# A two-block transformer on one core: starting the second block's stages with a pair of weight units in token layout, tile by tile

## The reference

```python
h = h + 0.5 * rmsnorm_2(swiglu(rmsnorm_2(h, g[0]), ffn1_w_in[i], ffn1_w_out[i]), g[1])
u = rmsnorm_2(h, g[2])
mix = even_mixer(u, ...) if i % 2 == 0 else odd_mixer(u, ...)
h = h + rmsnorm_2(mix, g[3])
h = h + 0.5 * rmsnorm_2(swiglu(rmsnorm_2(h, g[4]), ffn2_w_in[i], ffn2_w_out[i]), g[5])
gate = jax.nn.sigmoid(h @ ple_w_gate[i])
h = h + rmsnorm_2(gate * (p[i] @ ple_w_proj[i]), g[6])
```

## Time and profile before

| | |
|---|---|
| runs, us | 1816.14, 1817.77, 1819.4; median 1817.77 |
| span of the profiled execution, us | 1812.1; no time of its own beside it is given |
| PE busy | 1772.9 us, 98% |
| DVE, ACT busy | 952.5 us, 53%; 718.8 us, 40% |
| mean granted clock of PE | 0.998 of full speed |
| chain that ended last | PE 86%, DVE 7%, ACT 4%, DMA 1% |

### The profile page before, as it was taken

The page is one execution under the profiler, slowest core; times in us unless marked ns, Lnnn a source line. Parts: engine busy times, 40 slices in busy tenths (PEclk is TensorE's granted clock), DMA queues, the critical chain, the costliest instruction groups (busy, mean ns, idle before and its releaser), DMA issues.

```text
span 1812.1 us, 24884 instructions
## 1 busy us (share of the span) xinstructions
PE 1772.9 (98%) x9912; PEld 1349.9 (74%) x9912; DVE 952.5 (53%) x1200; ACT 718.8 (40%) x949; POOL 41.3 (2%) x55
## 2 busy tenths in 40 slices
PE   9999999999999999999999999999999999999997
PEld 8886454444545488888988888788887879888886
DVE  6584111111111275665776566675666854566665
ACT  5562111111111254435665344653445345444444
POOL 2000000000000000000000000000000001200000
PEclk9999999999999999999999999999999999999999
DMA  9367899999999955554435555545555554555551
GB/s 291 105 251 304 333 423 422 422 422 422 421 422 422 362 197 186 186 187 153 140 115 182 186 185 186 187 151 190 189 189 166 180 168 140 202 164 186 185 186 58
DMA packets 191205, 428.75 MB, mean 237 GB/s; under 512 B 7292, under 2 KB 145632, under 8 KB 166560
## 3 DMA queue, kind: packets, MB, share of 16 engines
q1 hardware_dynamic: 187952, 418.41, 63.5%
q0 software_dynamic: 3184, 9.36, 1.6%
HBM read 426.69 MB, written 1.05 MB: 236 GB/s over the span
## 4 chain that ended last, share of the span: by engine, by line
PE 86%; DVE 7%; ACT 4%; DMA 1%; issue 1%; DVEq 0%; SPq 0%; POOL 0%; ACTq 0%
PE pw L494 62%; PE acc L494 22%; DVE wl L1716 2%; DMA raw<-in_w_in 1%; PE pw L856 1%; ACT arena L1387 1%; DVE x L2158 0%; ACT sm L1379 0%; ACT wh L1214 0%; ACT arena L1495 0%; DVE scr L2170 0%; ACT L1238 0%; DVE scr L2227 0%; ACT arena L1514 0%; DMA cB<-in_decays 0%
## 5 line engine op out<-in xcount | busy, mean ns | idle before, releaser
L494 PE MATMUL pw<-aa,wh 128*128 128x512 f32 (+1 forms) x2384 | 702.4, 359 | 5.1 <-DVE aa L1726 2.7
L494 PE MATMUL pw<-aa,wl 128*128 128x256 f32 x1960 | 551.3, 281 | 0.0
L1716 DVE TENSOR_TENSOR wl<-raw,wh 128x2048 fp32r<-128x2048 f32 x205 | 463.2, 2297 | 110.5 <-ACT wh L1214 107.6
L494 PEld LDWEIGHTS pw<-aa,wh 128*128 128x128 f32 x2384 | 421.5, 190 | 82.3 <-DVE wl L1716 4.6
L1214 ACT ACTIVATE wh<-raw 128x2048 fp32r<-128x2048 f32 x205 | 380.9, 1906 | 51.4 <-DMA raw<-in_odd_w_in 28.5
L494 PEld LDWEIGHTS pw<-aa,wl 128*128 128x128 f32 x1960 | 371.9, 190 | 1.4
L494 PE MATMUL acc<-wh,aa 128*128 128x512 f32 x1088 | 347.0, 392 | 5.7 <-DVE aa L1734 3.5
L494 PE MATMUL pw<-mring,arena 128*64 128x512 f32 x1520 | 334.9, 595 | 5.4 <-issue 5.4
L494 PEld LDWEIGHTS pw<-mring,arena 128*64 128x64 f32 x1520 | 107.4, 137 | 206.7 <-issue 204.4
L494 PEld LDWEIGHTS acc<-wh,aa 128*128 128x128 f32 x1088 | 204.2, 188 | 52.1 <-DVE wl L1716 3.9
L494 PE MATMUL acc<-wl,aa 128*128 128x512 f32 x544 | 212.0, 390 | 0.0
(11 more groups left out here) (408 smaller groups left out, 1250.5 us busy)
## 6 DMA issues: line engine op xcount, KB each, us to landing
raw<-in_ffn_w_in SPq DMA_DIRECT2D x88, 1024.0 KB, 5.1
mring<-in_w_ed SPq DMA_DIRECT2D x64, 1024.0 KB, 16.4
mring<-in_w_eg SPq DMA_DIRECT2D x63, 1024.0 KB, 16.1
mring<-in_w_eu SPq DMA_DIRECT2D x63, 1024.0 KB, 18.1
raw<-in_ffn_w_out SPq DMA_DIRECT2D x44, 1024.0 KB, 5.0
raw<-in_odd_w_in SPq DMA_DIRECT2D x24, 1024.0 KB, 5.2
raw<-in_w_in SPq DMA_DIRECT2D x12, 1024.0 KB, 10.3
raw<-in_even_w_in SPq DMA_DIRECT2D x11, 1024.0 KB, 5.5
```

What stands on the lines that cost most here:

```text
L494: return pe.matmul(out, lhs, rhs, start=start, stop=stop, skip_group_check=True)
L1716: dve.tensor_tensor(wl[:, u % RING, :], raw[:, u % RING, :], wh[:, u % RING, :].bitcast(F32), ALU.subtract).then_inc(sig(f"{ep}_lo"), 1)
```

## The change

From the second stage on that starts with a norm after a tile-wise product (both stages of feed-forward two, feed-forward one of layer 1 and the odd mixer), the first two weight units are computed as a pair in token layout: activations stationary, 512 weight columns of two units streamed, tile 0 first, then tile 1 (`turn_tile`, `pair_tile`). High and low parts are made for one tile at a time, 128 columns an instruction, and those of tile 0 are written in between tile 1's norm steps. The matmuls of zeros are gone there. In the feed-forwards the pair is gate and up of the first block; its activation is done in token layout and turned by four transposes. In the odd mixer the pair is the values of head 0 (`ODD_ORDER`), copied out by ACT. The embedding stage does embeddings, turning and gates tile by tile; tile 0's gates end before tile 1's begin, and x of tile 0 is squared and normed before tile 1's sigmoid.

```diff
-        ODD_ORDER = (0, 1, 2, 3, 4, 5, 6, 7, 16, 8, 9, 10, 11, 12, 13, 14, 15, 17, 18, 19, 20, 21, 22, 23)
+        ODD_ORDER = (9, 8, 0, 1, 2, 3, 4, 5, 6, 7, 16, 10, 11, 12, 13, 14, 15, 17, 18, 19, 20, 21, 22, 23)
...
+            def turn_tile(t, spare):
+
+                w.more("diag_ready")
+                for c in range(KC):
+                    last = mm(tile_turned(t, c, spare), x[:, t, c * P:(c + 1) * P], diag[:, t, :])
+                    if c in (0, 1, 4, 7):
+                        last.then_inc(sig("turned"), 1)
+
+            def pair_tile(ep, u, t, bank, slots):
+
+                unit_ready(ep, u + 1)
+                out = pw[:, bank + t, :].rearrange("p (a n) -> p a n", a=2)
+                for k in range(KC):
+                    w.more("act_ready")
+                    last = mm3(out, ah[:, k, tok(t)], al[:, k, tok(t)], wh[:, slots, k * 256:(k + 1) * 256],
+                               wl[:, slots, k * 256:(k + 1) * 256], k == 0, k == KC - 1)
+                return last
...
-                turn_normed({0: (29, 0), 2: (28, 0)}.get(idx, (0, 14)))
-                pairs_of("b", u0, 0, arriving=True).then_inc(sig("b_used"), 1)
-                pairs_of("b", u0 + 1, 2).then_inc(sig("b_used"), 1)
...
+                    slots = slice(u0 % RING, u0 % RING + 2)
+                    turn_tile(0, 0)
+                    pair_tile("b", u0, 0, 2, slots).then_inc(sig("psum_for_act"), 1)
+                    turn_tile(1, 0)
+                    pair_tile("b", u0, 1, 2, slots).then_inc(sig("b_used"), 2)
...
+                    if by_tile:
+                        w.more("dve_for_pe", 2)
+                        for c in range(2):
+                            for t in range(NT):
+                                turned = pe.transpose(acc[:, 0, c * T + t * P:c * T + (t + 1) * P], hid_rows[:, t, c * P:(c + 1) * P], ident)
+                        turned.then_inc(sig("psum_for_act"), 1)
...
                 w.more("act_ready")
-                rows("b", UB[(l, "ple_proj")], 12, True, True, final=True, dst=pw, tile="proj_tile")
-                w.more("x_ready")
...
+                weighted(v0, 12, 0, pw[:, 0:2, :], True, True).then_inc(sig("psum_for_act"), 1)
+                w.more("dve_for_pe")
+                turn_plain(0)
+                weighted(v0, 12, 1, pw[:, 2:4, :], True, True).then_inc(sig("b_used"), 1)
+                w.more("dve_for_pe")
+                w.more("pp_ready")
+                turn_plain(1)
+                w.more("act_ready", KC)
+                for j in range(4):
+                    last = weighted(v0 + 1 + j, 2 * j, 0, acc[:, 0:2, :], j == 0, j == 3)
+                last.then_inc(sig("first_tile"), 1)
+                for j in range(4):
+                    w.more("act_ready", 2)
+                    weighted(v0 + 1 + j, 2 * j, 1, acc[:, 2:4, :], j == 0, j == 3).then_inc(sig("b_used"), 1)
...
+                slots = slice(0, RING, RING - 1)
+                turn_tile(0, 2)
+                pair_tile("b", u0, 0, 0, slots)
+                turn_tile(1, 2)
+                pair_tile("b", u0, 1, 0, slots).then_inc(sig("b_used"), 2)
...
-                for p in range(8):
-                    if p >= 2:
+                for p in range(2, 10):
+                    if p == 3:
+                        w.more("proj_evac")
+                    if p >= 4:
                         w.more("qk_evac")
...
+            def high_tile(t, chunks, col, spare):
+
+                for c in chunks:
+                    if c in (0, 1, 2, 5):
+                        w.more("turned")
+                    act.activation(ah[:, c, tok(t)], tile_turned(t, c, spare), ACT.Copy, scale=col(c)).then_inc(sig("high"), 1)
...
+                    split("b", u0 + 2)
+                    split("b", u0 + 3)
+                    for t in range(NT):
+                        if t == 0:
+                            w.more("psum_for_act")
+                        else:
+                            used("b", u0 + 1)
+                        act.activation(gate_tok[:, t, :], pw[:, 2 + t, 0:256], ACT.Silu).then_inc(sig("act_for_dve"), 1)
+                    split("b", u0 + 4)
...
+                        if between:
+                            high_tile(0, (half,), col, spare)
                     sum_root(t, factor)
                     if normed:
-                        square_x(t)
+                        squares_of_x(t)
+                        if between:
+                            high_tile(0, (2, 3, 4), col, spare)
+                        sum_root(t)
+                        if between:
+                            high_tile(0, (5, 6, 7), col, spare)
+                if col is not None:
+                    high_tile(1, range(KC), col, spare)
...
-                    if j == 11:
-                        evac_go(8, 0)
+                    if j == 5:
+                        evac_v(0)
                     if j == 13:
-                        evac_v(0)
+                        evac_go(10, 2)
...
+            def low_tile(t, chunks, col, spare):
+
+                for c in chunks:
+                    if c in (0, 1, 2, 5):
+                        w.more("high", 1 if c < 2 else 3)
+                    dve.scalar_tensor_tensor(al[:, c, tok(t)], tile_turned(t, c, spare), col(c), rd[:, c, tok(t)], ALU.mult,
+                                             ALU.subtract).then_inc(sig("act_ready"), 1)
...
                     if normed:
-                        diagonal(t)
...
+                        sum_halves(t)
+                        if between:
+                            low_tile(0, (2, 3, 4), col, spare)
+                        rstd(t)
+                        dve.tensor_scalar(diag[:, t, :], ident, sm[:, 14 + t:15 + t], None, ALU.mult).then_inc(sig("diag_ready"), 1)
+                        if between:
+                            low_tile(0, (5, 6, 7), col, spare)
```

More of the change, by code:

```diff
@@ L991, in ple, with weighted @@
[L991 to L994, removed]
+                v0 = UB[(l, "ple_proj")]
+                def weighted(u, chunk, t, dst, start, stop):
+                    unit_ready("b", u)
+                    s = u % RING
+                    for kk in range(2):
+                        for half in range(2):
+                            c = kk * D + half * 512
+                            last = mm3(dst[:, half, :], ah[:, chunk + kk, tok(t)], al[:, chunk + kk, tok(t)], wh[:, s, c:c + 512],
+                                       wl[:, s, c:c + 512], start and kk == 0, stop and kk == 1)
+                    return last
@@ L1496, in residual_rms, with squares_of_x, gated_rms @@
                                        accum_out=sm[:, 152 + 2 * t + half:153 + 2 * t + half]).then_inc(sig("squares"), 1)
+                        if between:
+                            high_tile(0, (half,), col, spare)
                     sum_root(t, factor)
                     if normed:
-                        square_x(t)
-            def gated_rms(u, normed):
+                        squares_of_x(t)
[6 more added lines that the diff above has]
+                    high_tile(1, range(KC), col, spare)
+            def squares_of_x(t):
+                for half in range(2):
+                    w.more("x_new")
+                    part = slice(half * 512, (half + 1) * 512)
+                    act.activation(junk[:, t, part], x[:, t, part], ACT.Square,
+                                   accum_out=sm[:, 152 + 2 * t + half:153 + 2 * t + half]).then_inc(sig("squares"), 1)
+            def gated_rms(u, col=None):
                 for t in range(NT):
+                    between = col is not None and t == 1
                     act.activation(sm[:, 158:159], cst("tie")[:, 0:1], ACT.Sigmoid)
@@ L2149, in ahead @@
                     split("b", u + j)
-            def norm_in(col, late=None):
-                if late is not None:
-                    split("b", late)
-                lows(col)
             def normed_half(t, h):
@@ L2209, in add_gated @@
                             dve.sem_inc(sig("out_ready"), 1)
-                if normed:
-                    w.more("x_new", 4)
-                    for t in range(NT):
-                        diagonal(t)
+                    if between:
+                        low_tile(0, (2, 3, 4), col, 0)
+                    if normed:
+                        w.more("x_new", 2)
+                        sum_halves(t)
+                        rstd(t)
+                        dve.tensor_scalar(diag[:, t, :], ident, sm[:, 14 + t:15 + t], None, ALU.mult).then_inc(sig("diag_ready"), 1)
+                        if between:
+                            low_tile(0, (5, 6, 7), col, 0)
+                if col is not None:
+                    low_tile(1, range(KC), col, 0)
             def ffn(l, n, idx):
-                u0, done = UB[(l, f"ffn{n}")], idx * FB
-                norm_in(lambda c: norm_col(l, 4 * (n - 1), c))
-                if l == 0 and n == 1:
+                u0 = UB[(l, f"ffn{n}")]
```

(2 more changed lines are left out.)

237 lines of the change are left out of this document (147 added, 90 removed).

## The result

The changed kernel has a median of 1820.47 us (12 runs, 1816.48 to 1823.85), the kernel before 1816.93 us (12 runs). The ratio is 1.0018, 95% interval 1.0011 to 1.0025: 3.3 us slower, where -1.1 us was forecast.

The account below looks back on a forecast made before the run. TensorE was taken as the bound, so only joints between stages count. Terms -4.4 (B, C), -2.2 (F, G), +1.0 (A, E), +2.8 and +1.7 (D) sum to -1.1 us: 1816.7 us, range 1810.2 to 1822.6.

Parts of the forecast that it names:

- D: Joint from feed-forward to odd mixer: PE stands 6.2 us before the fourth unit; 2.8 us lost, plus 1.7 for the clock.
- A: Joint from mixer to second feed-forward, layer 0: 0.5 us lost, nothing for the clock.
- C: Joint from embedding stage to layer 1's feed-forward: third unit starts earlier; gains 4.4 us together with B.
- E: Joint like A, in layer 1: 0.5 us lost, nothing for the clock.
- Rival 2: Clock falls at A, C and E too, 1.7 us each, giving 1821.8 us; chance 0.20.
- the prediction's own sign of being wrong: Wrong if D lacks a wait over 3 us, three joints have low clock, or A and E's third unit doesn't wait.
- B: Joint from feed-forward to embedding stage, layer 0: PE's wait before the gates goes; gains 1.7 us.
- F: Joint like B, in layer 1: gains 1.75 us, 2.2 us together with G.
- G: The end: gains the 0.4 us of the late sigmoid, 2.2 us together with F.

Follow-up runs that it names:

- silu_late: Changed kernel with ScalarE's table load for the gates moved behind the third unit's split at A, C and E; ratio 0.9990 to the kernel before.
- again: Changed kernel unaltered, measured once more beside other kernels; ratio 1.0014 to the kernel before.
- all3: Changed kernel with the edits of zeros, d_ahead and silu_late together; ratio 0.9928 to the kernel before.
- zeros: Changed kernel with matmuls of zeros again in the short gaps at A, C, D and E; ratio 0.9990 to the kernel before.
- d_zeros: Kernel zeros plus 24 matmuls of zeros in D's long wait ahead of the fourth unit; ratio 0.9986 to the kernel before.
- bare: Kernel before without its matmuls of zeros at the second block's five norm joints; ratio 1.0030 to the kernel before.
- emb_only: Kernel before with only the changed kernel's tile-by-tile embedding stage; ratio 0.9969 to the kernel before.
- d_ahead: Changed kernel with the fourth unit's split and the first pair's copy ahead of the sines at D; ratio 0.9978 to the kernel before.

## Why the prediction was wrong

The step that failed is "I put half of 3.4 us, 1.7, on D, and nothing on the others". The clock fell at A and C in both profiles of the changed kernel, and at E in that of silu_late; over the runs the changed kernel has 0.0043 less mean clock than before (0.0038 in the run again, beside it), some 4 to 4.6 half-clock stretches a run, of which A, C and the two at D are four. Rival 2, at 0.20, is what happened, as far as two of its three joints, and the prediction's own sign of being wrong, a low clock at three or more joints, came with D's. Its size (1.7 a joint) was nearly right: 1.70 at A, 1.33 at C, 1.6 at E (silu_late against all3). A and C make 3.0 us of the 4.4 by which the forecast missed, and zeros in the gaps gave back 4.4 to 5.1. I had read the wait on y_lo in the earlier trace rows, where the clock held through 2.2 us, as a gap that is safe. The changed kernel's first profile has a half-clock stretch behind that very wait (627.9), in code that the change didn't touch, and so have five others of the thirteen profiles, each with the same wait: a gap that held once was a draw, not a bound.

The other terms, each by a run in which the clock at the joint was as forecast:

- A and E, +0.5 each: 0.0 and +0.4 (zeros; 193.67 and 193.71 against 193.65 and 193.31). PE's gap before chunk 2 (2.15 us for 2.5) and the third unit's wait (1.27 for 1.5) came nearly as worked out.
- B and C, -4.4: -4.05 (zeros). B alone: from the last row of the feed-forward to the first gate 7.36 us (1147.77 to 1155.13) against 9.14, so 1.78 for the 1.7.
- F and G, -2.2: -2.07.
- D, +2.8 and +1.7 for the clock: +4.4, nearly the sum, by the mechanism named: angles late by tile 1's highs, three splits, then the copy. Split otherwise: d_zeros, without a half-clock stretch, still has +3.6, of which some 1 us is the slower stream of the last section.

Without the clock at A, C and E the sum was -1.1, a ratio of 0.9994; the run zeros, which is that case, has 0.9990. The terms missed by 0.1 to 0.5 us each and in both directions, so that the sum came so close is in part luck. But the order of the work was read rightly from the trace, and one resource that the old code paid for was counted as free.

The Trainium skill ("TensorE: Matmul & The Clock Gate", section "Why this matters for your kernels") warns only of idle gaps between bursts of matmuls that are longer than those at A and C. The traces differ from it, and the measurement decides: here the clock fell behind 2.15 and 1.94 us, and behind the 3.31 us at the bare kernel's D it held.

The absolute number rested on 5.7 us around the span; it is 2.0, and the rest was a short execution. The forecast of a difference doesn't hang on that, the comparison of two profiles does.

## What to carry to other kernels

Work that looks idle, such as matmuls of zeros, can be what holds the clock: before it is taken out, ask of each place how long PE will stand there, and where the traces show that gaps of that length can let the clock fall (here 2 us), price each as a half-clock stretch, even if one held. When tile 0's work is slid into tile 1's chain, look at what stands on ACT and DVE between the last result and the next weight's split: here a table load, three splits and six 128-column steps stood there; moving them and filling the gaps that stayed made a kernel 1.0% faster than before out of one that was 0.2% slower. Compare two profiles joint by joint against several of the same program, not by their spans.

## What was not expected of the hardware

The length of a gap doesn't decide alone whether the clock falls: behind three equal gaps of 3.31 us it fell twice, behind 2.15 us at A it fell where at E it held, and behind the wait of 2.26 us on y_lo it fell in six of thirteen profiles. What decides stays open.

The same stream of matmuls in the odd mixer, 512 and 256 columns in turn, ran at two rates at a granted clock of 1.00 without any wait, from behind joint D to the end of the stream: 16 matmuls in 2.77 us in before, the changed kernel (both times), zeros and silu_late, in 2.83 us in emb_only, bare and all kernels with an edit that takes D's half-clock stretches away. Two windows of 22.2 us show it, of the changed kernel and of d_ahead:

```profile
1412.00:1434.20 22.20, 22.20 (x130) 1.00 0.59 190
```

```profile
1405.00:1427.20 22.20, 22.20 (x127) 1.00 0.59 189
```

Over the stage of some 45 us the second is 1 us slower. In the changed kernel the third unit, ahead of the half-clock stretch at D, still ran at 2.81 to 2.83 us, so the rate changed within one program, across that stretch. But before, emb_only and bare do the same work there with no such stretch and differ all the same, so it isn't the whole cause; what is stays open and wasn't tried. It took about 1 us of what d_zeros and d_ahead would have gained.
